# RWKV scan of a hybrid trunk: products of token tiles put into the off-diagonal quarters of the array, and issued between the pairs of the inversion

## The reference

```python
def _rwkv7_scan(r, w, k, v, kk, a, S0):
    def step(S, inp):
        r_t, w_t, k_t, v_t, kk_t, a_t = inp
        sa = jnp.einsum('bhvk,bhk->bhv', S, kk_t)
        S = (S * w_t[:, :, None, :] - sa[..., None] * (kk_t * a_t)[:, :, None, :]
             + v_t[..., None] * k_t[:, :, None, :])
        return S, jnp.einsum('bhvk,bhk->bhv', S, r_t)
    xs = tuple(jnp.moveaxis(t, 1, 0) for t in (r, w, k, v, kk, a))
    S, o = lax.scan(step, S0.astype(jnp.float32), xs)
    return jnp.moveaxis(o, 0, 1), S
```

## Time and profile before

| | |
|---|---|
| time, median of 3 runs (lowest, highest) | 2422.75 us (2417.28, 2430.12) |
| the profiled execution's own time | 2419.26 us |
| its span in the profile | 2417.5 us |
| PE busy, share of the span | 2106.9 us, 87% |
| DVE, ACT, POOL busy | 1490.1, 959.9, 535.1 us |
| first scan, from the first L718 to the last L1032 | 208.5 to 380.8 us, 172.3 us |
| second scan | 1921.3 to 2101.5 us, 180.2 us |

### The profile page before, as it was taken

How to read it: one execution, slowest core, us unless ns; L and a number is a source line. 1 busy time by engine, 2 the same in 40 slices (tenths; PEclk the granted TensorE clock), 3 DMA queues, 4 the chain that set the end, 5 groups by cost and what they waited for, 6 DMA issues and landing times.

```text
span 2417.5 us, 54792 instructions
## 1 busy us (share of the span) xinstructions
PE 2106.9 (87%) x23495; PEld 1939.3 (80%) x23495; DVE 1490.1 (62%) x2234; ACT 959.9 (40%) x1640; POOL 535.1 (22%) x931
## 2 busy tenths in 40 slices
PE   4986996899989789799989697999798599879997
PEld 4955985899968677699989676999787389669997
DVE  4546534599467655589655775896555634358973
ACT  3341123455446601555445335555333311335543
POOL 7000000155114221046201540452000000003630
PEclk8987998999989888899999888999899689989999
DMA  4410111354433323244435262454343001223542
GB/s 125 150 62 2 30 36 49 106 174 153 150 112 107 118 73 102 79 157 158 161 124 158 71 181 79 148 167 162 116 129 104 3 21 30 65 70 124 172 158 79
DMA packets 272064, 257.77 MB, mean 107 GB/s; under 512 B 30692, under 2 KB 267206, under 8 KB 271822
## 3 DMA queue, kind: packets, MB, share of 16 engines
q1 hardware_dynamic: 221520, 219.63, 28.2%
q10 hardware_dynamic: 45774, 20.31, 3.1%
q0 software_dynamic: 4528, 14.33, 2.2%
HBM read 235.69 MB, written 18.54 MB: 105 GB/s over the span
## 4 chain that ended last, share of the span: by engine, by line
PE 52%; DVE 6%; ACT 3%; issue 2%; ACTq 1%; POOL 0%; DMA 0%; DVEq 0%; POOLq 0%
PE wide L525 6%; PE bank L525 6%; PE wide L526 6%; PE wide L527 6%; PE bank L527 6%; PE bank L526 6%; DVE arena L2338 3%; PE wide L536 2%; PE wide L740 1%; PE wide L755 1%; ACT arena L1603 1%; DVE arena L2335 1%; PE wide L752 1%; ACT w_hi L1603 1%; PE wide L547 1%
## 5 line engine op out<-in xcount | busy, mean ns | idle before, releaser
L2338 DVE TENSOR_TENSOR w_lo<-ring,w_hi 128x2048 fp32r<-128x2048 f32 (+1 forms) x208 | 471.0, 2268 | 322.9 <-ACT w_hi L1603 320.3
L525 PE MATMUL wide<-arena_rounded,w_hi 128*128 128x288 f32 x1632 | 495.5, 304 | 74.5 <-DVE arena_rounded L2338 57.6
L525 PE MATMUL bank<-arena_rounded,w_hi 128*128 128x288 f32 x1632 | 495.1, 303 | 32.4 <-issue 17.0
L526 PE MATMUL bank<-arena_rounded,w_hi 128*128 128x288 f32 x1632 | 490.4, 300 | 0.0
L527 PE MATMUL bank<-arena_rounded,w_lo 128*128 128x288 f32 x1632 | 489.2, 300 | 0.0
L526 PE MATMUL wide<-arena_rounded,w_hi 128*128 128x288 f32 x1632 | 488.8, 300 | 0.0
L527 PE MATMUL wide<-arena_rounded,w_lo 128*128 128x288 f32 x1632 | 487.1, 298 | 0.0
L1603 ACT ACTIVATE w_hi<-ring 128x2048 fp32r<-128x2048 f32 (+1 forms) x208 | 391.3, 1883 | 139.0 <-PE bank L527 71.4
L525 PEld LDWEIGHTS wide<-arena_rounded,w_hi 128*128 128x128 f32 x1632 | 313.5, 192 | 85.9 <-issue 81.5
L525 PEld LDWEIGHTS bank<-arena_rounded,w_hi 128*128 128x128 f32 x1632 | 315.4, 193 | 35.4 <-issue 31.3
L2335 DVE SCALAR_TENSOR_TENSOR arena<-arena,pv 128x304 f32<-128x304 f32 (+3 forms) x528 | 311.0, 599 | 36.4 <-PE wide L527 20.6
(11 more groups left out here) (476 smaller groups left out, 2739.2 us busy)
## 6 DMA issues: line engine op xcount, KB each, us to landing
ring<-in_ffn_w_up SPq DMA_DIRECT2D x88, 1024.0 KB, 5.1
ring<-in_ffn_w_down SPq DMA_DIRECT2D x32, 896.0 KB, 4.9
ring<-in_rwkv_w_rkv SPq DMA_DIRECT2D x24, 1024.0 KB, 5.3
ring<-in_ffn_w_down SPq DMA_DIRECT2D x16, 1024.0 KB, 5.2
ring<-in_gdn_w_in SPq DMA_DIRECT2D x16, 1024.0 KB, 5.8
ring<-in_hgrn_w_in SPq DMA_DIRECT2D x16, 1024.0 KB, 5.5
ring<-in_rwkv_w_o SPq DMA_DIRECT2D x8, 1024.0 KB, 5.2
sraw<-in_state_rwkv_wkv POOLq DMA_DIRECT2D x32, 128.0 KB, 3.1
```

The lines of the kernel that those rows point to most:

```text
L525: nc.tensor.matmul(out, wh, xh, start=first, stop=False)
L526: nc.tensor.matmul(out, wh, xl, start=False, stop=False)
L2338: return V.tensor_tensor(out, a, b, op)
```

## The change

1. **Places.** New names `TOK = (HALF[1], HALF[0])` and `TOKQ`: every product that goes from channels to tokens, or from tokens to channels, now writes to the other partition half than the one it reads. Its tile is off the diagonal of the array. Products from tokens to tokens and from channels to channels stay on it.
2. **Weaving.** Fill units are generators that yield "pair" after each of their steps, "last" before the last one and "unit" at the end. In `levels64(..., woven=True)` the levels call `pair()` between their own pairs, so that one fill step stands behind each of them, and `rest()` at the end of a D unit, in the middle and at the end of an E unit, which brings the fill unit to its end. A fill unit's wait stands where the unit begins, and that is now behind the first pair of the level's unit.
3. **Chain.** The products with the values (`from_values`) come first and alone, then those with the state (`from_state`) are added to the same bank 4; the state read (`read_state`) is issued before the solution, into bank 5, and `read_values` adds to it. A chunk with n > 0 has six units in place of four.
4. **Sample pairs.** Both halves (p = 0, 1) of the products with the values, of L1008 and of L1019/L1022 are issued together into two banks, as one step.
5. **Banks.** E units use 2 and 3, the second Gram matrix a spare bank. The state transfers of the samples use the other half (`TOK[hh]`); VectorE's and ScalarE's `yield`s follow.

```diff
+        TOK = (HALF[1], HALF[0])
+        TOKQ = (QUARTER[1], QUARTER[0])
...
             def levels64(tt_, names_, between, woven=False):
+                at = {"now": "unit"}
+                def pair():
+                    if woven and at["now"] in ("unit", "pair"):
+                        at["now"] = next(between, "end")
+                        assert at["now"] != "unit"
+                def rest():
+                    if not woven:
+                        unit(between)
+                        return
+                    while at["now"] in ("pair", "last"):
+                        at["now"] = next(between, "end")
...
                                 mm = nc.tensor.matmul(bk[b][rows, c * 64:c * 64 + 64], LT[g][rows, c, :], TF[g][rows, c, :],
                                                       start=True, stop=True)
+                            if c < KC - 1:
+                                pair()
                         mm.then_inc(filled["vector"], 1)
                         ke[g] = result("vector", b)
-                        next(between, None)
+                        rest()
                     for g in range(2):
-                        b = 4 + g
+                        b = 2 + g if woven else 4 + g
...
+                                pair()
                             for rows in HALF:
                                 mm = nc.tensor.matmul(bk[b][rows, 256 + c * 32:288 + c * 32].rearrange("p (b t) -> p b t", t=h),
                                                       EL[g][rows, c, :], halves(tt_[g][rows, c, :], h, 1), start=True, stop=True)
+                            if woven and c == 3:
+                                rest()
+                            elif c < KC - 1:
+                                pair()
...
+            def woven(emit, n):
+                for i in range(n):
+                    if i == n - 1:
+                        yield "last"
+                    emit(i)
+                    if i < n - 1:
+                        yield "pair"
...
                 for src in (V_, K_, B_):
                     b = spare()
                     pe.wait_ge(*freed(b))
-                    for c in range(KC):
-                        for rows in HALF:
-                            mm = nc.tensor.matmul(bk[b][rows, c * 64:c * 64 + 64], src[rows, c, chunk(n)], ident[rows, rows],
-                                                  start=True, stop=True)
-                    mm.then_inc(filled["scalar"], 1)
+                    def turned(c):
+                        for hh, rows in enumerate(HALF):
+                            last_mm["mm"] = nc.tensor.matmul(bk[b][TOK[hh], c * 64:c * 64 + 64], src[rows, c, chunk(n)],
+                                                             ident[rows, rows], start=True, stop=True)
+                    yield from woven(turned, KC)
+                    last_mm["mm"].then_inc(filled["scalar"], 1)
...
+                yield from woven(from_values, KC)
                 if n:
+                    last_mm["mm"].then_inc(signal("values_added"), 1)
+                    yield "unit"
+                    pe.wait_ge(sem("values_added"), after(pe, "values_added"))
+                    pe.wait_ge(sem("state_ready"), after(pe, "state_ready"))
...
+                yield "last"
+                for p in range(2):
+                    for hh in range(2):
+                        rows = TOKQ[hh][p]
+                        nc.tensor.matmul(bk[bs[p]][HALF[hh], :], sVK[rows, 1, m, :], spread[rows, 0, :], start=True, stop=False)
+                for p in range(2):
+                    for hh in range(2):
+                        rows = TOKQ[hh][p]
+                        mm = nc.tensor.matmul(bk[bs[p]][HALF[hh], :], sB[rows, m, :], spread[rows, 1, :], start=False, stop=True)
+                    mm.then_inc(filled["vector"], 1)
+                    result("vector", bs[p])
+                yield "unit"
                 for p in range(2):
                     pe.wait_ge(sem("sample_state_new"), after(pe, "sample_state_new"))
```

More of the change, by code:

```diff
@@ new lines, in chain, with read_state @@
+                k = result("scalar", 4)
+                yield "unit"
+                if n:
+                    pe.wait_ge(*freed(5))
+                    def read_state(c):
+                        for rows in HALF:
+                            last_mm["mm"] = nc.tensor.matmul(bk[5][rows, c * 64:c * 64 + 64], s0[rows, c, :], ARp[rows, c, n, 1, :],
+                                                             start=(c == 0), stop=False)
+                    yield from woven(read_state, KC)
+                    last_mm["mm"].then_inc(signal("state_read"), 1)
+                    yield "unit"
@@ new lines, in chain, with read_values @@
+                yield from woven(update, KC)
+                last_mm["mm"].then_inc(filled["vector"], 1)
+                result("vector", b)
+                yield "unit"
+                if n:
+                    pe.wait_ge(sem("state_read"), after(pe, "state_read"))
+                else:
+                    pe.wait_ge(*freed(5))
+                def read_values(c):
+                    for hh in range(2):
+                        rows = TOK[hh]
+                        nc.tensor.matmul(bk[5][HALF[hh], c * 64:c * 64 + 64], Vt[rows, c, :], KAR[n % 2][rows, c, 1, :],
+                                         start=(n == 0), stop=False)
+                    for hh in range(2):
+                        rows = TOK[hh]
+                        last_mm["mm"] = nc.tensor.matmul(bk[5][HALF[hh], c * 64:c * 64 + 64], US[rows, c, :], NRB[n % 2][rows, c, :],
+                                                         start=False, stop=(n == 0 or c == KC - 1))
@@ L982, in sample_pair @@
+                    yield from woven(read, NB)
+                    last_mm["mm"].then_inc(filled["scalar"], 1)
+                    k = result("scalar", bs[p])
+                    yield "unit"
                 pe.wait_ge(drained["scalar"], k + 1)
@@ L1006, in sample_pair @@
+                yield "unit"
+                pe.wait_ge(sem("values_spread"), after(pe, "values_spread"))
+                bs = [spare(), spare()]
+                for b in bs:
                     pe.wait_ge(*freed(b))
+                yield "last"
+                for p in range(2):
                     for hh in range(2):
-                        mm = nc.tensor.matmul(bk[b][HALF[hh], 0:NS], sU[QUARTER[hh][p], :], sNRB[QUARTER[hh][p], m, :],
-                                              start=True, stop=True)
@@ L2591, in levels64 @@
                     for g in range(2):
+                        if woven:
+                            next(between, None)
                         dve.wait_ge(filled["vector"], take())
```

333 lines of the change are left out of this document (173 added, 160 removed).

## The result

The changed kernel takes 2394.8 us (median of 4 runs, 2390.1 to 2398.7) against 2420.4 for the kernel before (4 runs): ratio 0.989, 95% interval 0.985 to 0.992. So it is faster, by 26 us where 44 were forecast (2377, between 2352 and 2412). The profiled execution took 2398.65 us, 20.6 less than the one before.

What follows compares the result with a forecast made beforehand. It took TensorE to bound the scans, with VectorE having room. Per scan -25.7 - 5.4 + 3.2 + 7.0 = -20.9 us, -41.8 for two, and about 2 more for half clock: -44, forecast 2377 us, range 2352 to 2412.

Steps and rivals of the forecast that it cites:

- Hidden pairs: In each scan, 220 off-diagonal fill steps run beside the levels' diagonal pairs, saving 0.117 us each: 25.7 us less.
- Spread: Sample pairs, m = 0, 1, 2: both halves together take about as long as one, 5.4 us less per scan.
- Tile sizes: Sample_begin's steps woven with 64x64 pairs: 23 more changes of tile size at 0.14 us, 3.2 us more per scan.
- New waits: In the scans, woven fill units no longer cover VectorE's and ScalarE's work: 7.0 us more per scan, bounds 0 and 14.
- (c): Turned-back states, L1022 to L1032: only one pair now lies between, so TensorE waits for VectorE, 5.7 us more per scan.
- Sum: All terms: -20.9 us per scan, -41.8 for two; about 2 us more from removed half-clock work: -44.
- Rival 1: In the scans, pairs hide but waits (14 us) and woven steps at 0.14 us eat half: 2403; chance 0.16.
- Rival 2: Clock: stalls bring half clock to both scans, 2387 to 2397, or a fuller array avoids it, 2367; chance 0.07 either way.
- Rivals 3 and 4: Woven steps: same-row loads and matmuls take turns, 2531 (chance 0.07); or quarters run one after the other, 2429 (0.08).

Runs made afterwards that it cites:

- Burst 9: Kernel before, products put ahead of its first scan, results unused: 64 steps of a 64x64 pair and four 64x32 products; 0.509 us per step.
- the bursts: Kernel before with nine series of products ahead of its first scan, waiting for nothing, results unused; 256 products need 14 us, 64 need 3.5, whatever the tile.
- bursts 3 and 4: Kernel before, products put ahead of its first scan: 128 pairs sharing their rows, then 128 sharing their columns; 15.2 us each, 0.119 per pair.
- burst 5: Kernel before, products put ahead of its first scan: 128 steps of all four quarters with 128 moving columns; 28.6 us, no idle time.
- burst 6: Kernel before, products put ahead of its first scan: 128 steps of all four quarters with 64 moving columns; 27.2 us, 10 of them idle.

## Why the forecast was right in sign and too large by 18 us

*Hidden pairs, 25.7 per scan:* right. Woven steps take 0.117 us (the count of 220 steps is not measured by itself). With the spread (-5.4) and tile sizes (+3.2) the array terms sum to -27.9. Busy time fell by 23.6 in the first scan, where the clock's lower average costs 160 x 0.07 - 172 x 0.03 = 6 us: 29.6 without it. In the second, where that difference is under 1 us, it fell by 28.1.

*Spread, 5.4:* right by the run of its own (12 us for two scans).

*Tile sizes:* 0.14 per change was right, and better than its working: the rows give 0.26 + 1.03 - 0.117 - 0.94 = 0.23 for entering and leaving, not 0.28. Burst 9 takes 32.56 / 64 = 0.509 per step; without the changes it would be 0.234, which leaves 0.137 each. Sample_begin whole brought 11 us where my number for it was 8, but about 6 of them are the clock's by the estimate above.

*New waits, +7:* this is the step that failed in its mechanism, "fill units used to cover what VectorE and ScalarE need; woven ones don't". Its largest part (c) is there, 1.6 us at L1155. But all waits for other engines together fell by 1.7 and 1.2 us, because the scan before had waits of its own that went (1.8 us of L853 for ScalarE) and L1032 had waited for VectorE as well (2.4 us in each scan). The woven order on the diagonal says the same: its scans are no longer than the spread and the clock make them. In their place stands idle time of 13.0 and 15.8 us more that waits for no engine. Before, it was at 0.6 us because a pair per 0.117 needs 256 instructions in 3.7 us and gets them in 3.5: the old pace lay 8% under a limit that I did not look for. The page had the size of a transfer in its instruction queue (186 transfers, 3.05 MB), and a division would have shown that weaving asks for one in 1.9 us where 3.7 had been the fastest steady pace of pairs; how fast they can come only the bursts showed.

*Sum:* -27.9 - 1.7 + 13.0 + 6 (clock) = -10.6 in the first scan, measured -11.9; -27.9 - 1.2 + 15.8 + 0.7 = -12.6 in the second, measured -12.7. So of the 23 us by which the profiled execution misses -44, idle time is 12 (+25.9 where I had +14), and the clock nearly 9: it cost 6.7 where I counted on 2 us of gain, a loss that I had as a rival and not in the sum. Outside the scans the profiled execution lost 4 us, which no part of the change explains; over the profiled executions of eleven versions of the kernel that part varies from 2059 to 2074 us.

*Rival 1, 2403:* its size came nearer (2395 lies between), its mechanism was wrong: no new waits for engines, and woven steps at 0.117, not 0.14. That the result fell into my range at all is in part luck: the supply cost nearly what rival 1 gave to waits. *Rival 2:* half true. The first scan has 10.2 us at 0.50 from 246.9, again in a sample pair with few matmuls (x156), and its lower average cost 6 of the rival's 10 us; the second scan kept its stretch. A like stretch stands in the traces with whole units (243 to 252) and with sample_begin whole (244 to 254), so it isn't the weaving that brings it. *Rivals 3 and 4:* refuted by the step of 0.117. The Trainium skill ("TensorE: Matmul & The Clock Gate", Part 3, "The mechanism") says that a weight load overlaps a running matmul only where the row group differs; bursts 3 and 4 (15.21 us for pairs of one row group, 15.22 for pairs of two) don't agree.

## What to carry to other kernels

Before you fill idle parts of the array with more small products, divide: instructions per step by time per step, against what the instruction transfers have brought at most. Here that was 256 per 3.45 us, or 64 float32 products. If the work is already near it, put independent products into other quarters and leave the order alone first: here they overlapped at unit borders, and that version gained as much as the woven one. If idle time is put down to "issue" after a change of order, count the instructions from one such piece to the next: multiples of 256 point to their supply. And compare the granted clocks before you explain a difference of 5 or 10 us.

## What the runs showed of the hardware that I had not expected

- TensorE's instructions: one transfer of 16.4 KB holds 256, counted three times (12288 more made 48 more, 1792 fewer made 7 fewer, 944 fewer made 4 fewer). In bursts without waits 64 float32 products with 64 moving columns take 3.4 to 3.5 us in 64x64, 64x32 and 32x32 tiles alike, and idle pieces in a woven scan lie multiples of 256 instructions apart.
- Whole units in different quarters overlap at their borders by up to 0.2 us: products of the later unit start ahead of the last ones of the unit issued before it.
- One float32 transpose among 64x64 products: 0.44 us per step in place of 0.117.
- The burst in one quarter alone ran at a granted clock of 0.50 for all of its 27.6 us, and the one with sixteen 32x32 tiles and gaps averaged 0.56; all four 64x64 quarters ran at 1.00, without gaps (burst 5) and with them (burst 6).
